# Value projections of a two-branch mixer layer as seven block products, with five low parts on VectorE

## What is computed

```python
proj = einsum('bld,dn->bln', x, w_in) + b_in
qa, fa, ia, za, qb, kb, vb, zb, qi, ki, wi, ga, gb = split(proj, cuts)
oa = rms_norm(hgrn2_mix(qa, fa, ia, lb)) * norm_a_g          # 4 heads of 128, recurrence
ob = dsa_mix(qb, kb, vb, qi, ki, wi, rel_bias)               # 8 heads of 64, top-128 keys of an indexer
ua = (oa * silu(za)) @ w_up_a;   ub = (ob * silu(zb)) @ w_up_b
y  = (sigmoid(ga) * ua + sigmoid(gb) * ub) @ w_out
out = layer_norm(ALPHA * x + y, ln_g, ln_b)
```

## Time and profile before

| | us |
|---|---|
| median of 3 runs | 460.01 |
| lowest, highest | 454.6, 460.18 |
| profiled execution, its own time | 454.26 |
| its span in the profile | 452.4 |
| TensorE busy | 444.5 |
| VectorE busy | 308.3 |
| ScalarE busy | 237.1 |
| GpSimd busy | 172.7 |

### The profile page before, as it was taken

One profiled execution on the slowest core, in us unless ns is written; L12 is line 12 of the kernel. 1 busy time (PEld: TensorE's weight loads), 2 busy tenths in 40 slices (PEclk: granted clock), 3 DMA queues, 4 the chain that ended last, 5 costly groups with the idle time before them and its releaser, 6 DMA issues.

```text
span 452.4 us, 7707 instructions
## 1 busy us (share of the span) xinstructions
PE 444.5 (98%) x2946; PEld 363.5 (80%) x2946; DVE 308.3 (68%) x586; ACT 237.1 (52%) x399; POOL 172.7 (38%) x171
## 2 busy tenths in 40 slices
PE   9999999999999999999999999999999999999994
PEld 7778888888888878888878887888788888778883
DVE  4546589999999855246889994891370057887676
ACT  5745445253236745384958656844594273335431
POOL 0444432583168822673006010000055453055955
PEclk9999999999999999999999999999999999999998
DMA  8808122257022794203221995022039354235013
GB/s 264 297 12 294 72 91 94 93 139 233 1 92 46 178 373 152 66 29 99 88 95 23 220 260 152 3 96 94 0 100 374 113 185 169 91 146 220 0 46 139
DMA packets 17859, 59.26 MB, mean 131 GB/s; under 512 B 2616, under 2 KB 4448, under 8 KB 16352
## 3 DMA queue, kind: packets, MB, share of 16 engines
q1 hardware_dynamic: 17008, 54.39, 35.7%
q0 software_dynamic: 576, 4.19, 4.7%
q10 hardware_dynamic: 240, 0.20, 0.1%
HBM read 54.57 MB, written 10.50 MB: 144 GB/s over the span
## 4 chain that ended last, share of the span: by engine, by line
PE 93%; DVE 4%; ACT 1%; issue 1%; POOL 0%; DVEq 0%; POOLq 0%
PE bank L641 22%; PE bank L642 22%; PE bank L643 22%; PE bank L974 3%; PE bank L971 3%; PE bank L973 3%; PE bank L804 2%; PE bank L789 2%; PE bank L887 2%; PE bank L840 2%; PE bank L780 1%; PE bank L779 1%; PE bank L931 1%; PE bank L769 1%; PE bank L768 1%; PE bank L685 1%
## 5 line engine op out<-in xcount | busy, mean ns | idle before, releaser
L1972 POOL TENSOR_TENSOR w_lo<-w_raw,w_hi 128x512 fp32r<-128x512 f32 x72 | 94.7, 1341 | 141.7 <-ACT w_hi L982 141.7
L641 PE MATMUL bank<-x_hi,w_hi 128*128 128x512 f32 x336 | 133.0, 396 | 0.0
L642 PE MATMUL bank<-x_lo,w_hi 128*128 128x512 f32 x336 | 131.2, 390 | 0.0
L643 PE MATMUL bank<-x_hi,w_lo 128*128 128x512 f32 x336 | 130.9, 390 | 0.0
L641 PEld LDWEIGHTS bank<-x_hi,w_hi 128*128 128x128 f32 x336 | 63.1, 188 | 13.9 <-issue 0.8
L643 PEld LDWEIGHTS bank<-x_hi,w_lo 128*128 128x128 f32 x336 | 63.1, 188 | 13.6
L642 PEld LDWEIGHTS bank<-x_lo,w_hi 128*128 128x128 f32 x336 | 63.1, 188 | 12.2
L982 ACT ACTIVATE w_hi<-w_raw 128x1024 fp32r<-128x1024 f32 (+2 forms) x63 | 62.3, 1011 | 3.3 <-PE bank L643 1.7
L1704 DVE TENSOR_TENSOR w_lo<-w_raw,w_hi 128x512 fp32r<-128x512 f32 x44 | 28.1, 683 | 27.9 <-ACT w_hi L982 27.9
L1069 ACT ACTIVATE prob<-prob,nmax 128x128 f32<-128x128 f32 (+3 forms) x32 | 17.7, 555 | 41.6 <-DVE nmax L1524 41.5
L1500 DVE MAX8 best<-score 128x8 f32<-128x256 f32 (+2 forms) x48 | 26.8, 559 | 1.1
(11 more groups left out here) (269 smaller groups left out, 808.5 us busy)
## 6 DMA issues: line engine op xcount, KB each, us to landing
w_raw<-in_w_units SPq DMA_DIRECT2D x58, 512.0 KB, 5.0
out_t<-in_w_units POOLq DMA_DIRECT2D x2, 1024.0 KB, 11.2
out_t<-out_t POOLq DMA_DIRECT2D x2, 1024.0 KB, 10.4
z_b<-out_t SPq DMA_DIRECT2D x2, 1024.0 KB, 5.8
y_sb<-in_x_tok SPq DMA_DIRECT2D x4, 512.0 KB, 5.2
out<-y_sb SPq DMA_DIRECT2D x8, 256.0 KB, 2.0
x_raw_hi<-in_x_t SPq DMA_DIRECT2D x4, 256.0 KB, 5.1
x_raw_lo<-in_x_t SPq DMA_DIRECT2D x4, 256.0 KB, 5.8
```

What stands on the lines that cost most here:

```text
L641: nc.tensor.matmul(dst, a_hi, b_hi, start=first, stop=False)
L642: nc.tensor.matmul(dst, a_hi, b_lo, start=False, stop=False)
L643: return nc.tensor.matmul(dst, a_lo, b_hi, start=False, stop=last)
L1972: nc.gpsimd.tensor_tensor(split_target(u, kiwi_lo, x_lo, w_lo)[:, k, :], raw(u)[:, k, :], split_target(u, kiwi_hi, x_hi, w_hi)[:, k, :].bi ...
```

## The change

The values of both branches are now one product: X times the 1024 columns [vb | ia]. X is cut into four blocks (tokens by channels), the weights into four (channels by branch), and seven block products b11, b21, t1, t2, t3, t4, b22 give all of it. Each block is a unit of its own of two quarters, one per bank (128 tokens by 512 columns, 12 matmuls), put between normal units. The four weight sums t1 to t4 are made in DRAM by DMAs (`begin_sum` on SP, `add_vi_block` on GpSimd's queue); the four X sums are made by VectorE (`sum_x`), rounded by ScalarE (`round_x_sum`), and their rest taken by VectorE (`x_sum_lo`). Low parts of b11 and b21 stay with GpSimd; those of t1, t2, t3, t4 and b22 go to VectorE. Evictions combine the products (`leave_block`). The item phase moves from quarter 39 to 50, the tree by 6 quarters, `gb0` and `gb1` are kept raw until the merge. NQ, the number of quarters, is 122.

```diff
-UNITS = ["kiwi", "qi0", "qi1", "zb0", "zb1", "za0", "za1", "qb0", "kb0", "vb0", "vb1", "qb1", "kb1",
-         "ia0", "ia1", "fa0", "fa1", "qa0", "qa1", "ga0", "ga1", "ga2", "ga3",
+UNITS = ["kiwi", "qi0", "qi1", "zb0", "b11", "b21", "zb1", "t1", "za0", "t2", "za1", "t3", "qb0", "t4", "kb0",
+         "b22", "qb1", "kb1", "fa0", "fa1", "qa0", "qa1", "ga0", "ga1", "ga2", "ga3",
          "gb0", "gb1", "gb2", "gb3", "up0", "up1", "up2", "up3"]
...
+QUARTERS = [2 if n in VI_BLOCKS else 4 for n in UNITS]
...
-Q_ITEM = [39 + 2 * (i // 2) if i < 16 else 55 + 4 * ((i - 16) // 2) // 3 for i in range(len(ITEMS))]
+Q_ITEM = [(50, 61)[i // 16] + 4 * (i % 16 // 2) // 3 for i in range(len(ITEMS))]
...
-Q_PREP = (64, 68)
-Q_NEAR = (72, 81)
-Q_TREE = (73, 83)
+Q_PREP = (70, 74)
+Q_NEAR = (78, 87)
+Q_TREE = (79, 89)
...
-LO_DVE = (*range(Q_PREP[0] // 4 + 1, Q_MERGE // 4 + 2), *(UNITS.index(f"up{i}") for i in range(1, 4)))
+LO_DVE = (*(UNITS.index(n) for n in ("t1", "t2", "t3", "t4", "b22")), *range(UNITS.index("ga0"), UNITS.index("up0")), *(UNITS.index(f"up{i}") for i in range(1, 4)))
...
+VI_SUMS_AT = {12: "t1", 13: "t3", 17: "t2", 22: "t4"}
+X_HI_AT = {13: 0, 25: 1, 26: 2, 27: 3}
+X_LO_AT = {15: 0, 26: 1, 28: 2, 30: 3}
...
-    for b, first, per in ((1, 18, 1.7), (2, 28, 1.7), (3, 38, 1.5)):
+    for b, first, per in ((1, 18, 1.7), (2, 28, 1.7), (3, 39, 1.3)):
...
+                if UNITS[u] in OUT_SUMS and a == 0:
+                    sp.wait_ge(sum_done[UNITS[u]], 16)
...
-            def quarter_joint(u, n):
...
+            def quarter_block(u, i):
+
+                name = UNITS[u]
+                wait_bank(u, i)
+                first = name != "b21"
+                if i == 0 and name in X_OF:
+                    pe.wait_ge(s_lo_done, X_OF[name] + 1)
+                w = slot(u)
+                b_hi, b_lo = by_pairs(w_hi[:, w, :, :]), by_pairs(w_lo[:, w, :, :])
+                dst = proj_bank[i][:]
+                for j in range(PAIRS):
+                    if i == 0:
+                        wait_lo(pe, u, j + 1)
+                    a_hi, a_lo = vi_stationary(name, j, i)
+                    nc.tensor.matmul(dst, a_hi, b_hi[:, j, :], start=first and j == 0, stop=False,
+                                     skip_group_check=True)
+                    nc.tensor.matmul(dst, a_hi, b_lo[:, j, :], start=False, stop=False, skip_group_check=True)
+                    mm = nc.tensor.matmul(dst, a_lo, b_hi[:, j, :], start=False, stop=j == PAIRS - 1,
+                                          skip_group_check=True)
+                mm.then_inc(part_done, 1)
...
+            def leave_block(name, i):
+
+                bank, v_low, a_up = proj_bank[i][:], v_b[:, 2 + i, :], v_a[:, i, :]
+                if name == "b11":
+                    ins = nc.vector.tensor_tensor(v_low, bank, bias_vb[:], ALU.add)
+                elif name == "b21":
+                    ins = nc.vector.tensor_tensor(v_b[:, i, :], bank, bias_vb[:], ALU.add)
...
+                elif name == "t3":
+                    link(nc.vector.tensor_tensor(v_a[:, 2 + i, :], a_up, bank, ALU.subtract))
+                    ins = nc.vector.tensor_tensor(v_low, bank, v_low, ALU.add)
...
+                ins.then_inc(proj_out[i], 1)
+                if name == "t2":
+                    wait_proj_out(dve, "t2", i)
+                    wait_proj_out(dve, "t1", i)
+                    link(nc.vector.tensor_tensor(a_up, a_up, v_low, ALU.subtract))
+
+            def sum_x():
+
+                a11, a12, a21, a22 = (x_part(r, h) for r in range(2) for h in range(2))
+                nc.vector.tensor_tensor(xs_raw[:, 0], a21, a22, ALU.subtract).then_inc(s_raw_done, 1)
...
+            def x_sum_lo(n):
+
+                dve.wait_ge(s_hi_done, n + 1)
+                nc.vector.tensor_tensor(xs_lo(n), xs_raw[:, n], xs_hi(n).bitcast(F32),
+                                        ALU.subtract).then_inc(s_lo_done, 1)
...
+            sum_x()
             dve.wait_ge(early_in, 32)
-            for q in range(4 * NMAIN):
+            for q in range(NQ):
                 side(q)
+                if q in X_LO_AT:
+                    x_sum_lo(X_LO_AT[q])
```

More of the change, by code:

```diff
@@ L61 @@
 OUT_WEIGHTS = ("b11", "b21", "t1", "t2", "b22", "t3", "t4")
+VI_BLOCKS = ("b11", "b21", "t1", "t2", "t3", "t4", "b22")
+QUARTERS = [2 if n in VI_BLOCKS else 4 for n in UNITS]
+STARTS = [sum(QUARTERS[:u]) for u in range(NMAIN + 1)]
+NQ = STARTS[NMAIN]
+AT = [(u, j) for u in range(NMAIN) for j in range(QUARTERS[u])]
+LEAVING = {}
+for _u in range(1, NMAIN):
+    for _i in range(2):
+        LEAVING.setdefault(STARTS[_u] + (_i + 1) * QUARTERS[_u] // 2, []).append((_u, _i))
 OUT_ORDER = tuple((n, i) for n in range(len(OUT_WEIGHTS)) for i in range(2))
@@ L159, in hybrid_kernel @@
             with ExitStack() as s2:
-                relus = sb("relus", [P, 2, SEQ], stack=s2)
-            q_lo_23 = sb("q_lo_23", [P, 2, SEQ], F32R, s)
+                q_hl = sb("q_hl", [P, HEADS_I, SEQ], F32R, s2)
+            with ExitStack() as s2:
+                xs_late = sb("xs_late", [P, 4, 4, HALF], F32R, s2)
+            q_hi_g1, q_lo_g1 = (sb(n, [P, 4, SEQ], F32R, s) for n in ("q_hi_g1", "q_lo_g1"))
             v_b = sb("v_b", [P, TB, D_B], stack=s)
@@ L351, in wait_split_target @@
             if last >= 1:
-                eng.wait_ge(part_done, parts(JOINT.get(last, last), 1))
+                eng.wait_ge(part_done, parts(last, 1))
         def parts(u, i):
@@ L536, in wait_dist, with leaving @@
             eng.wait_ge(dist_done, 6 * p + lv)
-        def part_out_at(q):
-            u, i = (q // 4 - 1, 1) if q % 4 == 0 else (q // 4, 0)
-            if u < 0 or q % 2 or not UNITS[u][2:].isdigit():
-                return None
-            return UNITS[u][:2], 2 * int(UNITS[u][2]) + i
+        def leaving(q):
+            return LEAVING.get(q, [])
         def merged_at(q):
-            part = part_out_at(q)
-            return part[1] if part and part[0] == "up" else None
+            return next((2 * int(UNITS[u][2]) + i for u, i in leaving(q) if UNITS[u].startswith("up")), None)
         def level_distance(engine, p, lv):
@@ L1005, in leave_bank @@
                 kind = name[:2]
-                if kind in ("vb", "ia", "up") or (name == "kiwi" and i == 1):
+                if name in VI_BLOCKS or kind == "up":
                     return
@@ L1023, in leave_bank @@
                 elif kind in ("qb", "kb"):
-                    if name == "qb0" and i == 0:
-                        act.wait_ge(row_out, 16)
                     if name == "kb0" and i == 0:
@@ L1919, in _ @@
                     split_first(j)
+            sum_x()
             dve.wait_ge(early_in, 32)
-            for q in range(4 * NMAIN):
+            for q in range(NQ):
                 side(q)
+                if q in X_LO_AT:
+                    x_sum_lo(X_LO_AT[q])
+                if q == 14:
+                    link(nc.vector.tensor_tensor(bias_ia[:], bias_ia[:], bias_vb[:], ALU.add))
                 if q == Q_ITEM[0] - 3:
@@ L2063, in scale_columns @@
                 nc.gpsimd.tensor_tensor(y_sb[:, t, c], y_sb[:, t, c], ln_gb[:, 1, c], ALU.add).then_inc(y_done[half in ON_POOL[t]], 1)
-            for q in range(4 * NMAIN):
+            for q in range(NQ):
                 side(q)
+                if q in VI_SUMS_AT:
+                    add_vi_block(VI_SUMS_AT[q])
                 if q in OUT_LO_AT:
```

242 lines of the change are left out of this document (158 added, 84 removed).

## The result

| | before | changed |
|---|---|---|
| median, us (runs) | 457.4 (4) | 492.2 (4) |
| lowest to highest | 454.6 to 460.2 | 490.9 to 496.5 |
| profiled execution, its span | 454.3, 452.4 | 492.0, 490.1 |
| mean granted clock | 0.997 | 0.969 |

The ratio is 1.078 (95%: 1.067 to 1.089): slower by 35 us, 25 more than the 467 predicted, and 15 past the end of the range. The comparisons ran on several chips, where the fastest run of the kernel before took 453.6 to 454.6, so that a difference between the medians of two changed kernels is good to about 1 us. A run more than 1.5% above the fastest of its kernel counts as slow and is left out of a ratio, which concerns three of the twelve runs of the last experiment.

The account below looks back on a forecast made before the run. TensorE's matmuls were taken as the bound, with VectorE second and lagging. From 454.3 us, less 5.4 for matmuls, plus 17.0 of waits on VectorE and 1.0 for GpSimd: 466.9, say 467; range 455 to 477.

Parts of the forecast that it names:

- TensorE's part: Joint units on TensorE: 24 matmuls fewer at 0.227 us each save 5.4 us, if nothing waits.
- VectorE's list: VectorE's work from first top-k round to kb0's second eviction: 101.4 us, done at 160.7, making TensorE wait 17.0 us.
- TensorE runs as before up to there: Stretch ahead of the first top-k round: unchanged, so that round starts at 59.28 us.
- The four X sums fall in the 5.02 us in which VectorE waits.: VectorE before 20.40 us: the sums, 4.9 us, fit its wait and were costed at nothing.
- The 8 further DMAs find engines with little to do.: Weight-sum transfers of 1 MB each: DMA share is 0.16 in 60 to 80 us, so costed at nothing.
- About a us each: GpSimd's queue: issuing four of the DMAs among its low parts takes about a us each.
- What I named as a danger: SP's queue: were the sum t1 late, SP's later weight loads would stand behind it; no size given.
- GpSimd's effect: 27 added two-SBUF-input VectorE instructions beside GpSimd: 1.0 us taken, 3.2 if placed at random, 0 if never together.
- The 0.47 per instruction: VectorE instructions reading two SBUF tiles: one overlapped by GpSimd's low parts loses up to 0.47 us.
- Lower bound, 0.9 us: The lower bound's steps in VectorE's work up to kb0's second eviction: 0.9 us.
- has slack: Item phase moved behind quarter 50 and raw gate values: slack covers them; 0 to 2 us allowed, 0 taken.
- Rival C: TensorE at 1.2 GHz, double pitch, after waits of 2 to 4 us, once to three times: 470 to 475; chance 0.16.

Follow-up runs that it names:

- e12: e11 with one of the sixteen top-k rounds of each query block (other penalties than the reference's): 452.3 us, ratio 0.991.
- e1: The changed kernel with the low parts of all seven blocks on GpSimd: 482.5 us, ratio 1.058.
- e11: e8 with the lower bound's chain one quarter earlier: 460.1 us, ratio 1.010.
- e2: The changed kernel with the four X sums moved from the start to quarters 9 and 11, two at each: 487.7 us, ratio 1.070.
- e3: The changed kernel without its eight DMAs for the weight sums, so values come from unsummed weights: 481.1 us, ratio 1.056.
- e15: The last experiment: the kernel before with the eight weight-sum transfers alone added, into memory that nobody reads: 461.4 us, ratio 1.007.
- e10: The changed kernel with the lower bound's chain alone one quarter earlier, on VectorE and ScalarE: 487.7 us, ratio 1.073.
- e13: e8 with the weight-sum transfers back, additions at quarters 14, 19, 24, 29, summed blocks one unit later, lower bound's chain one quarter earlier: 464.3 us.
- e14: e13 with top-k rounds from quarters 20, 31 and 43 at 1.5, 1.35 and 1.25 a quarter: 468.7 us, ratio 1.026.
- e8: The changed kernel with block low parts on GpSimd, X sums at quarters 9 and 11, no weight-sum DMAs, later top-k rounds: 465.9 us, ratio 1.027.

## Why the prediction was wrong

The direction, the engine and the manner were right: TensorE is the bound, its waits are mostly on VectorE's evictions between 60 and 185 us, and the matmuls saved are real. The size was wrong by 25 us. By its steps:

- **TensorE's part, 5.4 us.** Nearly right: 24 records fewer, and in e12 4.3 us less busy time and an end under the kernel before.
- **VectorE's list, 101.4 us from 59.28.** The list took 111.3 us, and it began at 71.47 us, 12.2 late, so it ended at 182.8 us instead of 160.7. These 22.1 us, and the some 2.6 of half clock behind its last wait, are nearly all of the 25. The start, "TensorE runs as before up to there", was the step that failed most. I had checked nothing ahead of 59 us but the one gap for the X sums. Inside the list VectorE's own waits came to 7.3 us where I took 1.3, its scores and masks to 3.3 us more than before, and the lower bound to 3.9 instead of 0.9. Of the list's own terms the low parts, 12.4, cost 9.8 (e1), nearly their size. That the rounds fill VectorE is shown by e11 against e12.
- **"The four X sums fall in the 5.02 us in which VectorE waits."** They took 8.0 us, not 4.9, since GpSimd's first low parts stand in the same gap. e2: 4.5 us.
- **"The 8 further DMAs find engines with little to do."** I took the DMA share of 60 to 80 us. SP issues the copies at 18.9, 37.6 and 39.5 us and GpSimd the additions from 43 us on, into a window with 0.48 before, now 1.02. e3: 11.2 us, of which e15 finds 3 to 7 without the short blocks. "About a us each" for GpSimd's issues left out VectorE: beside the first two of them one score took 5.61 us. What I named as a danger, SP's loads behind a late sum, happened once and cost nothing: SP waited 4.8 us for the sum t1, but ScalarE did not wait for that load. The load that held ScalarE was zb1's, issued at 48.9 us with no sum ahead of it and landed at 67 and 72.
- **GpSimd's effect, 1.0 us, bound 3.2.** I counted only the added instructions. The old ones suffered more: the 21 scores took 15.7 us before and 23.8 after, 8.1 more, and the X sums 3.2. The 0.47 per instruction was no upper bound either; one lost 5.1 in the changed kernel.
- **Lower bound, 0.9 us.** I priced its instructions and did not look at what stood ahead of ScalarE's half after the shift. It is a 5.2 us wait; undoing it gained 4.6 us in e10 and 5.8 in e11. Of the 0.9 itself two steps grew by 1.7 us beside GpSimd. That the item phase's shift "has slack" failed here.
- **Rival C, the clock.** Its mechanism came true as an addition to the forecast, not as an alternative: 9.4 to 13.8 us. My sum had it at nothing. I gave it one to three falls; the trace has five (at 26, 71, 98, 122 and 180 us), which show in six of the ten windows. The Trainium skill (TensorE: Matmul & The Clock Gate, "HAM oscillation") says that gaps between groups of matmuls put the array to half clock, and here the trace agrees: 5.28 us for twelve matmuls after such a gap, instead of 2.72.
- **The range.** Each cover that I trusted (gap, idle queues, slack) had been read for one edit at a time. Three of them failed at once, and five of the waits then brought the clock down.

What stays open: why the kernel before has two levels, and whether a whole version can end under it. The runs point to about 10 us of waits and clock left in e13, all on VectorE's list, in which two instructions beside GpSimd lost 4.0 and 3.0 us; no order that I tried took them away.

## What to carry to other kernels

When phases are moved by a constant, look at every pair of instructions on two engines that wait for each other, and at what now stands ahead of each in its queue: short steps priced by their durations can hide a wait for the very bank they hold up. Read the cover of a hidden cost (a gap, an idle queue) at the time when the new work runs, with all the other additions already in it. On an engine that bounds the kernel, price a wait of some us at the wait plus the half-clock stretch that may stand behind it. And where GpSimd issues DMAs among its own tensor instructions, look at what VectorE reads from SBUF beside them.

## What the hardware showed

- VectorE's instructions with two SBUF inputs lose up to about 1.2 us beside GpSimd's tensor instructions (128x1024 at 2.3 us instead of 1.22, four columns at 1.20 instead of 0.16). Where GpSimd's run follows one of its DMA issues without a pause, they can wait for the whole run (128x256 at 5.61 instead of 0.48, in e14 128x128 at 4.06 instead of 0.29). MAX8 and MATCH_REPLACE8 were not touched: medians of 561 and 542 ns before, 561 and 543 after, the longest 697 and 678, and 696 and 677.
- GpSimd loses as well: four 128x512 low parts took 7.96 us beside VectorE's sums, and 5.05 in the kernel before at 78 us.
- One and the same wait can bring TensorE's clock down or not. In e11 TensorE waited 2.02 us for q_lo, and the next matmuls started 0.43 us apart, with a granted clock of 0.91 at 120 to 140 us; in e8 it waited 2.01 us for the same eviction, they started 0.23 apart, and the clock was 1.00 (TensorE's timelines of e11 and of e8):

```profile
134.16 0.80 PE L786 MATMUL bank<-w_hi,x_hi 128*128 128x512 f32 x1 [2.02 <-DVE q_lo L1545]
134.76 0.63 PE L788 MATMUL bank<-w_lo,x_hi 128*128 128x512 f32 x1
135.19 0.63 PE L789 MATMUL bank<-w_hi,x_lo 128*128 128x512 f32 x1
```

```profile
134.65 0.50 PE L786 MATMUL bank<-w_hi,x_hi 128*128 128x512 f32 x1 [2.01 <-DVE q_lo L1545]
134.99 0.39 PE L788 MATMUL bank<-w_lo,x_hi 128*128 128x512 f32 x1
135.22 0.39 PE L789 MATMUL bank<-w_hi,x_lo 128*128 128x512 f32 x1
```

- With the sums in DRAM under way, the 512 KB loads of 40 to 80 us had a median of 14.5 us to landing and a longest of 22.9; in the kernel before the median there is 4.3.
